# Time mix of an RWKV-7 block: small fp32 products packed in the array, the gate ahead of the keys, a longer first token in the output product

## What is computed

```python
xx = jnp.pad(x, ((0, 0), (1, 0), (0, 0)))[:, :-1] - x
xr, xw, xk, xv, xa, xg = [x + xx * mu[i] for i in range(6)]
r, k, v = xr @ w_rkv[0], xk @ w_rkv[1], xv @ w_rkv[2]            # 1024x1024 each
w = -softplus(-(w_decay0 + tanh(xw @ w_decay1) @ w_decay2)) - 0.5  # rank 64
a = sigmoid(a0 + (xa @ a1) @ a2)                                   # rank 64
g = sigmoid(xg @ g1) @ g2                                          # rank 160 = 128 + 32
kk = heads(k * k_k)
kk = kk * rsqrt(maximum(sum(kk * kk, -1), 1e-24))                  # per head of 64
k = k * (1 + (a - 1) * k_a)
# scan over tokens: S = S * decay + (S @ -kk) (kk * a)^T + v k^T;  y = S @ r
y = group_norm(y) * gn_g + gn_b + bonus(r, k, r_k, v)
out = (y * g) @ w_o
```

## Time and profile before

| | us |
|---|---|
| median of 3 runs | 1489.75 |
| lowest and highest | 1488.91, 1490.53 |
| the profiled execution | 1488.55 |
| its span in the profile | 1486.8 |
| mean granted TensorE clock | 0.971 |

### The profile page before, as it was taken

The page is one execution under the profiler, slowest core; times in us unless marked ns, Lnnn a source line. Parts: engine busy times, 40 slices in busy tenths (PEclk is TensorE's granted clock), DMA queues, the critical chain, the costliest instruction groups (busy, mean ns, idle before and its releaser), DMA issues.

```text
span 1486.8 us, 27383 instructions
## 1 busy us (share of the span) xinstructions
PE 1404.9 (94%) x11125; PEld 1260.6 (85%) x11125; DVE 929.2 (62%) x1365; ACT 753.8 (51%) x1164; POOL 42.7 (3%) x79
## 2 busy tenths in 40 slices
PE   7979999899999899899998999999999998899998
PEld 5857989689999787899997898799997787799997
DVE  7818544667767665766776566755556566565554
ACT  6552322565556664655556554544444464454443
POOL 5000000010000000000000000100001000000000
PEclk9989999999999899999999999999999999999999
DMA  8320001755555432655554554456555552256550
GB/s 253 116 85 1 18 3 41 260 196 188 174 193 176 142 107 77 221 184 194 173 198 137 180 194 142 153 189 196 175 194 156 161 184 66 86 170 198 181 187 29
DMA packets 135073, 222.25 MB, mean 149 GB/s; under 512 B 6137, under 2 KB 105697, under 8 KB 134720
## 3 DMA queue, kind: packets, MB, share of 16 engines
q1 hardware_dynamic: 132688, 214.19, 43.7%
q0 software_dynamic: 2144, 6.61, 1.4%
q10 hardware_dynamic: 144, 0.06, 0.0%
HBM read 219.77 MB, written 1.05 MB: 149 GB/s over the span
## 4 chain that ended last, share of the span: by engine, by line
PE 86%; DVE 8%; ACT 4%; issue 2%; DMA 1%; ACTq 0%; DVEq 0%
PE ps L501 83%; DVE ulo L487 1%; DVE scratch L1884 1%; PE ps L797 1%; DVE x_sb L1858 1%; ACT uhi L479 1%; DVE scratch L2242 0%; PE ps L1147 0%; DVE xs L1834 0%; DVE xn_lo L1846 0%; ACT scratch L1375 0%; DVE x_sb L1864 0%; DMA raw<-in_w_rkv 0%; DMA scratch<-in_mu 0%; ACT xn_hi L1406 0%
## 5 line engine op out<-in xcount | busy, mean ns | idle before, releaser
L487 DVE TENSOR_TENSOR ulo<-raw,uhi 128x1024 fp32r<-128x1024 f32 x400 | 488.3, 1224 | 366.3 <-ACT uhi L479 365.6
L479 ACT ACTIVATE uhi<-raw 128x1024 fp32r<-128x1024 f32 x400 | 422.6, 1059 | 450.8 <-PE ps L501 435.0
L501 PE MATMUL ps<-xn_hi,uhi 128*128 128x256 f32 x1472 | 418.2, 284 | 6.6 <-DVE ulo L487 2.5
L501 PE MATMUL ps<-xn_lo,uhi 128*128 128x256 f32 x1472 | 416.5, 283 | 0.0
L501 PE MATMUL ps<-xn_hi,ulo 128*128 128x256 f32 x1472 | 416.5, 283 | 0.0
L501 PEld LDWEIGHTS ps<-xn_hi,uhi 128*128 128x128 f32 x1472 | 282.3, 192 | 10.5 <-DVE ulo L487 4.2
L501 PEld LDWEIGHTS ps<-xn_lo,uhi 128*128 128x128 f32 x1472 | 282.3, 192 | 1.7
L501 PEld LDWEIGHTS ps<-xn_hi,ulo 128*128 128x128 f32 x1472 | 282.3, 192 | 0.0
L501 PE MATMUL ps<-uhi,xm_hi 128*128 128x512 f32 x512 | 201.2, 393 | 1.8 <-DVE xm_lo L2190 1.1
L501 PE MATMUL ps<-ulo,xm_hi 128*128 128x512 f32 x512 | 200.6, 392 | 0.0
L501 PE MATMUL ps<-uhi,xm_lo 128*128 128x512 f32 x512 | 159.6, 390 | 0.0
(11 more groups left out here) (276 smaller groups left out, 1318.5 us busy)
## 6 DMA issues: line engine op xcount, KB each, us to landing
raw<-in_mlp_w SPq DMA_DIRECT2D x64, 1024.0 KB, 5.2
raw<-in_w_up SPq DMA_DIRECT2D x44, 1024.0 KB, 5.0
raw<-in_w_down SPq DMA_DIRECT2D x22, 1024.0 KB, 4.8
raw<-in_gmlp_w_in SPq DMA_DIRECT2D x16, 1024.0 KB, 5.3
raw<-in_fox_w_in SPq DMA_DIRECT2D x16, 1024.0 KB, 5.1
raw<-in_w_rkv SPq DMA_DIRECT2D x12, 1024.0 KB, 6.8
raw<-in_gmlp_w_out SPq DMA_DIRECT2D x8, 1024.0 KB, 4.9
raw<-in_w_o_rwkv SPq DMA_DIRECT2D x4, 1024.0 KB, 9.2
```

What stands on the lines that cost most here:

```text
L479: nc.scalar.activation(ring_unit(uhi, m, n), raw_unit(n, j), ACT.Copy).then_inc(hi_done, 1)
L487: nc.vector.tensor_tensor(ring_unit(ulo, m, n), raw_unit(n, j), ring_unit(uhi, m, n).bitcast(F32), ALU.subtract).then_inc(lo_done, 1)
L501: return nc.tensor.matmul(o, l, r, start=start, stop=stop, skip_group_check=True)
```

## The change

- **L1A** is loaded ahead of r's first slot. VectorE, not ScalarE, scales its weights by mu, for w and for a alike, and both first products become 16 matmuls of 128 columns (24 before). The mixed input for a (`mix(4)`) goes. ScalarE's `tanh` and copy come after the first roundings of r.
- **Second products of w and a** alternate between the two halves of the array's rows, w into banks 4 to 7, a into banks 0 to 3.
- **The gate** is made ahead of k. Its 32-column part goes to four column groups, which gives four partial sums; a product with `rep` adds them and puts the sum on four row groups, and the 32-row part of the second product uses the four row groups. `g2`'s last 32 rows are loaded four times.
- **Keys**: the exponentials come before `proj("k")`'s evictions. `head_sums` (32 columns, four column groups) goes in front of v's third unit, `spread` uses four row groups. `keys(q)` multiplies each pair of key tiles (512 columns) when it is evicted, in turn with the splits. The running sums are 8 scans of 256 instead of 32 of 64, with a mask of zeros at the chunk starts.
- **Scan stages**: `gain_gate` moves behind `sb` of pair 1, all of the first tile's group norm behind `x3` of pair 1. `w_o_rwkv` loads wait for `z2` of pair 1.
- **Output product**: 5 units for tile 0 ahead of tile 1. Units 27 and 28 are kept in `xm_hi` and `xm_lo`, outside the ring.

```diff
-    phase("r", [r[0], ("L1A",), *r[1:]])
+    phase("r", [("L1A",), *r])
...
-        head_cols = xs[:, 0, 0:P].rearrange("p (f h) -> p f h", h=H)
-        head_rows = xs[0:H, 1, :].rearrange("p (f c) -> p f c", c=P)
+        head_cols = xs[:, 0, 0:T].rearrange("p (f c) -> p f c", c=32)
+        head_rows = xs[:, 1, :].rearrange("p (f c) -> p f c", c=P)
+        k_squares = gb[:, 0:2, :].rearrange("p g (f t) -> p (g f) t", t=T)
...
+        O_AHEAD = [unit0(at["o"]) + RING, unit0(at["o"]) + RING + 1]
+
+        def ring_of(m):
+
+            if m not in O_AHEAD:
+                return uhi[:, m % RING, :], ulo[:, m % RING, :]
+            e = O_AHEAD.index(m)
+            return [b[:, 4 * e:4 * e + 4, :].rearrange("p f t -> p (f t)") for b in (xm_hi, xm_lo)]
+
...
-            if m >= RING:
+            if m >= RING and m not in O_AHEAD:
...
-                        sp.wait_ge(*[(lora_ps, 2), (lora2_ps, 8), (lora_ps, 4), (gate_ps, 2), (y_done, 3),
+                        sp.wait_ge(*[(lora_ps, 2), (lora2_ps, 4), (lora_ps, 4), (gate_ps, 2), (y_done, 3),
                                       (y_done, 3)][special.index(o)])
+                        if slots[o][0] == "L2":
+                            sp.wait_ge(lora2a_ps, 4)
                     else:
                         sp.wait_ge(lo_done, (0 if i is None else 12 * i) + unit0(o) + 2)
                     if at["v"] <= o < at["v"] + 4:
-                        sp.wait_ge(core_ps, stage_no[("u", 2, 1)] + 1)
+                        for g in range(2):
+                            k = stage_no[("z2", 1, g)]
+                            sp.wait_ge(moved[ring_bank[k][0]], ring_use[k][0])
...
 
-                for f in range(NF):
-                    last = mm(bank(b, T)[0:H, :], head_cols[:, f, :], sq[:, f, :], f == 0, f == NF - 1)
+                for e in range(2):
+                    for i in range(4):
+                        last = mm(bank(b, T)[32 * i:32 * i + 32, :], head_cols[:, 2 * i + e, :], sq[:, 2 * i + e, :],
+                                  e == 0, e == 1)
                 last.then_inc(fsum_ps, 1)
 
             def spread(row, b0, done):
 
-                for b in range(4):
-                    for t in range(2):
-                        last = mm(bank(b0 + b, T, T * t), head_rows[:, 2 * b + t, :], row, True, True)
-                    last.then_inc(done, 1)
+                for t in range(2):
+                    for i in range(4):
+                        r = slice(32 * i, 32 * i + 32)
+                        last = mm(bank(b0 + i, T, T * t), head_rows[r, 2 * i + t, :], row[r, :], True, True)
+                        if t == 1:
+                            last.then_inc(done, 1)
...
-                mm(bank(4, T)[0:64, :], l1a[:, 128 * k:128 * k + 64], hT[:, k, 1:T + 1], k == 0, False)
+                mm(bank(7, T), l1a[:, 128 * k:128 * k + 128], hT[:, k, 1:T + 1], k == 0, False)
             for k in range(NF):
                 if k == 0:
                     pe.wait_ge(lw_done, 1)
                 if k % 2 == 0:
                     pe.wait_ge(xx_done, k // 2 + 1)
-                last = mm(bank(4, T)[0:64, :], l1a[:, 1024 + 64 * k:1088 + 64 * k], f3(S(S_X))[:, k, :], False,
-                          k == NF - 1)
-            last.then_inc(lora_ps, 1)
-            for k in range(NF):
-                pe.wait_ge(lmix_done, k + 1)
-                last = mm(bank(1, T)[64:128, :], l1a[:, 128 * k + 64:128 * k + 128], f3(S(S_MB))[:, k, :], k == 0,
-                          k == NF - 1)
-            last.then_inc(lora_ps, 1)
+                last = mm(bank(7, T), l1a[:, 1024 + 128 * k:1152 + 128 * k], f3(S(S_X))[:, k, :], False, k == NF - 1)
+            last.then_inc(lora_ps, 2)
...
-            pe.wait_ge(lora_done, 1)
-            proj("r", 0, xn_hi, xn_lo, first_split=0, split_done=rlo_done)
+
+            def before_last_r():
+                pe.wait_ge(lora_done, 2)
+
+            proj("r", 0, xn_hi, xn_lo, first_split=0, split_done=rlo_done, last=before_last_r)
...
-            for j in range(2):
-                pe.wait_ge(lora_done, j + 1)
-                for q in range(4):
-                    pe.wait_ge(proj_done, 4 + 4 * j + q - 3)
-                    for t in range(2):
-                        f = 2 * q + t
+            for q in range(4):
+                pe.wait_ge(proj_done, q + 1)
+                if q == 2:
+                    pe.wait_ge(vec_done, 2)
+                for t in range(2):
+                    f = 2 * q + t
+                    for j, done in enumerate((lora2_ps, lora2a_ps)):
                         hj = slice(64 * j, 64 * j + 64)
-                        last = mm(bank(4 + q, T, T * t), l2[hj, P * f:P * f + P], lh[hj, :], True, True)
-                    last.then_inc(lora2_ps, 1)
+                        last = mm(bank(4 * (1 - j) + q, T, T * t), l2[hj, P * f:P * f + P], lh[hj, :], True, True)
+                        if t == 1:
+                            last.then_inc(done, 1)
             pe.wait_ge(landed[special[2] % RAW], landed_at(special[2]))
             pe.wait_ge(mix_done, 2)
-            pe.wait_ge(vec_done, 2)
-            for c0, c1 in ((0, 128), (128, 160)):
-                for k in range(NF):
-                    last = mm(bank(2 + c0 // 128, T)[0:c1 - c0, :], l1g[:, 160 * k + c0:160 * k + c1],
-                              f3(S(S_MB))[:, k, :], k == 0, k == NF - 1)
-                last.then_inc(lora_ps, 1)
-            pe.wait_ge(mixlo_done, 1)
-            proj("k", 12, xm_hi, xm_lo)
+            pe.wait_ge(proj_done, 5)
+            for k in range(NF):
+                last = mm(bank(4, T), l1g[:, 160 * k:160 * k + 128], f3(S(S_MB))[:, k, :], k == 0, k == NF - 1)
+            last.then_inc(lora_ps, 1)
+            pe.wait_ge(proj_done, 6)
+            for k in range(NF):
+                i = k % 4
+                last = mm(bank(5, T)[32 * i:32 * i + 32, :], l1g[:, 160 * k + 128:160 * k + 160],
+                          f3(S(S_MB))[:, k, :], k < 4, k >= 4)
+            last.then_inc(lora_ps, 1)
             pe.wait_ge(landed[special[3] % RAW], landed_at(special[3]))
-            pe.wait_ge(lora_done, 4)
+            pe.wait_ge(lora_done, 3)
+            pe.wait_ge(proj_done, 12)
             g2 = raw[:, special[3] % RAW, :]
             for tok in range(NT):
                 for half in range(2):
-                    o = acc(tok, half)
-                    mm(o, tg0[:, P * tok:P * tok + P], g2[:, 512 * half:512 * half + 512], True, False)
-                    last = mm(o, tg1[0:32, P * tok:P * tok + P], g2[0:32, 1024 + 512 * half:1536 + 512 * half],
-                              False, True)
+                    mm(acc(tok, half), tg0[:, P * tok:P * tok + P], g2[:, 512 * half:512 * half + 512], True, False)
+            pe.wait_ge(heads_built, 1)
+            pe.wait_ge(gpart_done, 1)
+            mm(bank(6, T), rep, lh[:, :], True, True).then_inc(lora_ps, 1)
+            pe.wait_ge(lora_done, 4)
+            for tok in range(NT):
+                for half in range(2):
+                    i = 2 * tok + half
+                    last = mm(acc(tok, half), tg1[32 * i:32 * i + 32, P * tok:P * tok + P],
+                              g2[32 * i:32 * i + 32, 1024:1536], False, True)
                 last.then_inc(gate_ps, 1)
-            pe.wait_ge(proj_done, 16)
-            pe.wait_ge(heads_built, 1)
-            head_sums(f3(S(S_H)), 4)
-
+            pe.wait_ge(mixlo_done, 1)
+            proj("k", 12, xm_hi, xm_lo)
             def before_v(k):
                 if k == 0:
                     pe.wait_ge(mixlo_done, 2)
                     pe.wait_ge(gate_done, 2)
+                if k == 2:
+                    pe.wait_ge(proj_done, 16)
+                    head_sums(k_squares, 4)
...
-                pe.wait_ge(xlo_done, 4 * tok + 2)
-                for j in range(3):
+                for j in range(5):
+                    if j % 4 == 0:
+                        pe.wait_ge(xlo_done, 4 * tok + (4 if j else 2))
                     if tok == 0:
                         pe.wait_ge(lo_done, m + j + 1)
-                    wh, wl = uhi[:, (m + j) % RING, :], ulo[:, (m + j) % RING, :]
+                    wh, wl = ring_of(m + j)
                     for half in range(2):
                         c = slice(512 * half, 512 * half + 512)
...
-            for k in range(3, NF - 2):
-                if k == 4:
-                    pe.wait_ge(xlo_done, 8)
-                d_unit(pe, m + k, xn_hi[:, k, :], xn_lo[:, k, :], False, False, base=4)
+            d_unit(pe, m + 5, xn_hi[:, 5, :], xn_lo[:, 5, :], False, False, base=4)
...
+            decays()
+            decays_back()
+            act.wait_ge(built, 2)
+            act.wait_ge(mixlo_done, 2)
+            proj("k", f3(S(S_K)), squares=k_squares, square_cols=V_KK, after={2: gates})
+            warm(ACT.Sqrt)
+            upto(21)
             act.wait_ge(ksum_done, 1)
             A_(k_norm, k_norm, ACT.Sqrt).then_inc(knorm_done, 1)
```

(50 more changed lines are left out.)

141 lines of the change are left out of this document (67 added, 74 removed).

## The result

| | before | changed kernel |
|---|---|---|
| median, us (4 runs each) | 1489.33 | 1452.12 |
| lowest and highest | 1488.73, 1490.53 | 1448.03, 1453.35 |
| span of the profiled execution | 1486.8 | 1449.4 |
| mean granted TensorE clock | 0.971 | 0.979 |

The ratio of the times is 0.9746 (95% interval 0.9733 to 0.976). The forecast was 1448.8, with 1440 to 1463 around it. The span fell by 37.4 us where the sum said 40.9.

The account below looks back on a forecast made before the run. TensorE carried 86% of the chain, so its waits and its clock were taken as the bound. Terms summing to -40.9 us took the profiled 1488.55 us to 1447.6; the median, 1.2 above, was 1448.8, range 1440 to 1463.

Parts of the forecast that it names:

- second products and gate: Stage after r, with packed matmuls taken to overlap 3.4-fold: 14.7 us instead of 23.1, -8.3 us.
- k: The k stage, with the exponentials ahead of its splits and 3.0 us of waits: 26.7 us, +1.9 us.
- the wait: TensorE's 7.20 us wait before head sums goes because v's second slot is free earlier: -7.1 us.
- scan: In the scan, hold-ups by VectorE go (-3.8) and half of the low-clock cost goes (-3.0): -6.8 us.
- output product: From the scan's end to the output's end: 24.3 us instead of 27.3, -3.0 us.
- new low clock, k and v: Waits in k can bring a new low-clock stretch, about 3 us each: 0 to +6, taken as +2 us.
- the 64x64 row: Earlier profile's scan matmuls on 64x64 tiles, 0.062 us each, read as 3.7-fold overlap; 3.4 was taken for the packed matmuls.
- splits come before they are needed: In r, VectorE loses eight mixes, so only unit 0's start-up wait stays: 24.0 us instead of 27.4.
- The rule weighed: The skill page says changing tiling mode drains TensorE; some ten changes estimated at 2.4 us, making the sum -38.5.
- the hold-ups go, -3.8: In the scan, TensorE's three waits for VectorE (0.76, 1.06, 1.97 us) disappear once gain_gate and group norm move: -3.8 us.
- wait 0.6: TensorE's wait counted within the output product's 24.3 us, with five units covering the second tile's group norm: 0.6 us.
- the rivals: Packing doesn't overlap (0.10), 1463; splits' k/v chain binds harder (0.13), 1460; v's load still late (0.02), 1461; slower (0.03), 1508.

Follow-up runs that it names:

- experiment 1: Changed kernel with the same packed matmuls in another order (two in a row per 32-wide tile, all of w before a): 1453.96 us, ratio 0.9771.
- experiment 3: Changed kernel with VectorE's gain_gate and first-tile group norm, and ScalarE's root, back in their old places in the scan: 1453.53 us, ratio 0.978.
- experiment 6: Kernel of experiment 5 with no split of the output's weights before the scan's end, loads still at z2: 1451.24 us.
- experiment 9: Kernel of experiment 5 with the loads back at u of pair 2 and early splits only for the first load's units: 1445.32 us, ratio 0.9701.
- experiment 5: Changed kernel with ScalarE's splits up to unit 28 ahead of its wait for the scan's end: 1448.04 us, ratio 0.9726.
- experiment 8: Kernel of experiment 5 with one load at z2, three behind later stages, and early splits only up to the second load: 1448.60 us, ratio 0.9737.
- experiments 4 and 10: Both on the changed kernel. 4: three units for the first output tile instead of five, 1455.75 us. 10: keys' multiplies moved behind k, 1461.58 us.

## Why the prediction was right, and where it wasn't

Step by step, forecast and measured in us:

| step | forecast | measured | from |
|---|---|---|---|
| start | -3.9 | -3.5 | first matmul 20.16 |
| r | -3.4 | -2.3 | 25.1 long |
| second products and gate | -8.3 | -9.1 | 14.0 long |
| k | +1.9 | +0.9 | 25.7 long |
| the wait | -7.1 | -7.2 | none left |
| head sums | -4.9 | -5.0 | 1.07 |
| v | -7.4 | -6.6 | 25.8 less head sums |
| up to the scan | -33.2 | -32.5 | 143.36 and 110.85 |
| scan | -6.8 | -3.4 | 120.3 |
| output product | -3.0 | -1.4 | 25.9 |
| new low clock, k and v | +2 | 0 | 1.00 in both |
| what follows | 0 | 0 | 1192.4 in both |
| sum | -40.9 | -37.4 | spans; the terms are rounded |

**Up to the scan** every step came within 1.1 us, and the misses partly cancel. Packing works as the 64x64 row suggested: 1.07 us for head sums against 1.1 taken, 3.73 for both second products against 3.7. In r a wait of 1.05 us for VectorE's roundings is left, which "splits come before they are needed" had passed over. The pairs in k have the pace that was worked out, but only two waits of the three (0.56 and 1.42) fall in k and the third (1.33) at v's first unit. So k was costed 1.0 too high and v 0.8 too low. (The forecast's waits in k, 0.8 and 2.4, went into its sum as 3.0.)

**The rule weighed.** The second products and gate took 14.0 us, less than the 14.7 that were summed without any drain, where the estimate by the Trainium skill, TensorEngine Tiling (Array Packing), Tiling Modes, had 2.4 us more over the whole change. The trace doesn't show the drain as a cost here; the only idle time that it names in this stretch is 0.47 us for the sigmoid. What order does is experiment 1.

**Scan: the step that failed is "the hold-ups go, -3.8".** They did go (experiment 3 brings them back), but 2.38 us came as a new wait behind the last of them, with a stretch of low clock. All bracketed waits of TensorE from 0.3 us up, from 157 in the changed kernel and its place before, come to 5.4 us before (0.76, 1.06, 0.50, 0.76, 1.97, 0.31) and 5.7 after (0.58, 0.66, 0.50, 0.77, 0.40, 2.38, 0.44). So the hold-ups brought nothing, and what the scan gained is the clock's: its loss is (1 - 0.92) x 123.7 = 9.9 us before and (1 - 0.96) x 120.3 = 4.8 after, 5.1 less, where 3.0 were taken. But TensorE's busy time in the scan fell by 3.5 us only (117.42 to 113.89). Clock share times length overstates the price of a low stretch: the same 30 matmuls take 1.6 us from start to next start at 0.50 in experiment 3 (215.16) and 0.94 at 1.00 in the changed kernel (212.94), 1.7 times and not twice. Whether that is the whole difference was not worked out. The text had looked for what is late next on VectorE and ScalarE and not on TensorE's own side. It had moved the loads 6 us and priced them by whether the splits wait for them, and that price was indeed nothing: ScalarE waits for the landing, but experiment 6 shows that taking these splits away changes nothing in TensorE's wait. What the loads do is hold back the next block of instructions (the table in experiment 9). With the loads late the scan comes to 9.0 us less than before, more than the 6.8 of the forecast; 1.8 of that is the shorter low stretch ahead of `z2`.

**Output product: the step that failed is "wait 0.6".** The chain of the second tile was counted with VectorE's work, without the split that ScalarE makes between the scan's end and VectorE's last one. Its price was 1.5 us, and experiment 5 has both it and the forecast's length.

**New low clock, +2,** didn't come in k and v: waits of up to 1.42 us left the clock at 1.00 there. It came behind the 2.38 (0.73), behind the 1.56 of experiment 8 (0.57 from 221 to 225) and, in experiments 4 and 10, behind waits of 4.00 and 3.57. None of the rivals came about: packed matmuls overlapped 3.4-fold as taken, the pairs lost nothing beyond the waits forecast, the v load is issued at 53.73, and the packed stages kept the full clock.

**Luck.** The time lies 3.3 us above the forecast, inside its range, but scan and output product together gave 4.9 us less than summed, half of their forecast. The 2 us set aside for low clock, which were not needed, hide part of that. "Under 25 us from the scan's end" was not met (25.9), and "clock near 1.00" not in the second of its two stretches.

**Open** stays why the loads at z2 hold the block back, and why one of them is enough for 1.56 us. Open is also when low clock comes: it differs between two executions of one kernel (experiment 9).

## What to carry to other kernels

Small plain-fp32 matmuls are cheap once they lie on different tiles of the array. Don't put long runs of them on one tile. What they free up is collected only if VectorE's multiplies are spread to where it has room. When a hold-up of TensorE is removed in dense small matmuls, its own next stretch is a candidate for what is late next. There, read in the DMA view when the blocks of instructions start, and try bulk loads behind the next one and not just ahead of it. And of a chain behind a barrier, list what each engine's program has between the barrier and the first step that counts, splits for somebody else included.
